# Stick-breaking attention inside a fused layer: value products issued two key blocks at a time, from two buffers of turned weights

## What is computed

```python
def stick_breaking_attention(q, k, v):          # 6 heads of 64, blocks of 128 queries
    for start in range(0, s_, Q_BLOCK):
        end = start + Q_BLOCK
        z = jnp.einsum('bqhd,bkhd->bhqk', q[:, start:end], k[:, :end]).astype(jnp.float32) * scale
        ...
        log_not = jnp.where(strict, jax.nn.log_sigmoid(-z), 0.0)
        tail = lax.cumsum(log_not, axis=3, reverse=True) - log_not
        weights = jnp.where(strict, jnp.exp(jax.nn.log_sigmoid(z) + tail), 0.0)
        outs.append(jnp.einsum('bhqk,bkhd->bqhd', weights.astype(v.dtype), v[:, :end]))

def ssd_chunked_scan(xs, dt, a, bm, cm):
    ...
    decay = jnp.where(causal, jnp.exp(jnp.where(causal, seg, 0.0)), 0.0)
```

## Time and profile before

| what | us |
|---|---|
| median of 3 runs | 1339.45 |
| lowest and highest of them | 1339.34, 1344.62 |
| the profiled execution, its own time | 1344.1 |
| its span in the trace | 1342.3 |
| the stretch of the attention's tasks | 71 to 354 |

### The profile page before, as it was taken

The page is one execution under the profiler, slowest core; times in us unless marked ns, Lnnn a source line. Parts: engine busy times, 40 slices in busy tenths (PEclk is TensorE's granted clock), DMA queues, the critical chain, the costliest instruction groups (busy, mean ns, idle before and its releaser), DMA issues.

```text
span 1342.3 us, 16727 instructions
## 1 busy us (share of the span) xinstructions
PE 1299.1 (97%) x6288; PEld 1027.5 (77%) x6288; DVE 841.8 (63%) x996; ACT 508.1 (38%) x778; POOL 227.7 (17%) x152
## 2 busy tenths in 40 slices
PE   6999999999989998999999999999999999999986
PEld 5776766777776887888888787878787787888886
DVE  4546645646388556423477777768676867677765
ACT  4435535547654225112333332424242333233421
POOL 0000000052310002500112111111112121211126
PEclk9999999999999998999999999999999999999998
DMA  5101000010003212111020111111120101011202
GB/s 232 47 32 32 32 32 32 32 48 16 1 16 111 79 49 95 60 32 47 16 79 32 63 40 55 47 47 63 47 77 33 63 31 63 31 63 47 94 32 95
DMA packets 22661, 71.97 MB, mean 54 GB/s; under 512 B 2512, under 2 KB 2768, under 8 KB 22608
## 3 DMA queue, kind: packets, MB, share of 16 engines
q1 hardware_dynamic: 22608, 71.22, 15.7%
HBM read 67.02 MB, written 4.19 MB: 53 GB/s over the span
## 4 chain that ended last, share of the span: by engine, by line
PE 72%; DVE 9%; ACT 3%; issue 2%; DMA 2%; DVEq 0%; SPq 0%; ACTq 0%
PE ps L696 13%; PE ps L698 13%; PE ps L697 13%; PE ps L1054 7%; PE ps L1055 7%; PE ps L1053 7%; PE ps L774 2%; PE ps L791 2%; DMA down_raw<-u_down 2%; DVE conv_ff L1864 1%; DVE w_lo L579 1%; PE ps L835 1%; PE ps L750 1%; ACT conv_ff L1454 1%; PE ps L1084 1%
## 5 line engine op out<-in xcount | busy, mean ns | idle before, releaser
L696 PE MATMUL ps<-x_hi,w_hi 128*128 128x512 f32 x336 | 140.1, 417 | 11.4 <-DVE x_lo L516 10.6
L698 PE MATMUL ps<-x_hi,w_lo 128*128 128x512 f32 x336 | 133.7, 398 | 0.0
L697 PE MATMUL ps<-x_lo,w_hi 128*128 128x512 f32 x336 | 133.5, 397 | 0.0
L1916 DVE TENSOR_TENSOR acc<-acc,ps 128x512 f32<-128x512 f32 x144 | 96.2, 685 | 53.0 <-PE ps L698 52.5
L1054 PE MATMUL ps<-mix_lo,w_hi 128*128 128x512 f32 x320 | 126.7, 396 | 0.0
L1053 PE MATMUL ps<-mix_hi,w_hi 128*128 128x512 f32 x320 | 126.7, 396 | 0.0
L1055 PE MATMUL ps<-mix_hi,w_lo 128*128 128x512 f32 x320 | 126.7, 396 | 0.0
L696 PE MATMUL ps<-h_hi,w_hi 128*128 128x512 f32 x288 | 114.8, 399 | 1.6 <-DVE acc L1916 1.6
L698 PE MATMUL ps<-h_hi,w_lo 128*128 128x512 f32 x288 | 114.1, 396 | 0.0
L697 PE MATMUL ps<-h_lo,w_hi 128*128 128x512 f32 x288 | 114.0, 396 | 0.0
L2191 POOL TENSOR_TENSOR weight_sums<-raw 128x512 f32<-128x512 f32 x20 | 29.1, 1456 | 494.2 <-DMA raw<-u_up 494.2
(11 more groups left out here) (263 smaller groups left out, 2841.5 us busy)
## 6 DMA issues: line engine op xcount, KB each, us to landing
raw<-u_up SPq DMA_DIRECT2D x44, 512.0 KB, 3.3
raw<-u_in SPq DMA_DIRECT2D x22, 512.0 KB, 3.3
down_raw<-u_down SPq DMA_DIRECT2D x40, 256.0 KB, 2.8
x_stage<-u_x SPq DMA_DIRECT2D x8, 512.0 KB, 7.8
raw<-u_out SPq DMA_DIRECT2D x8, 512.0 KB, 3.2
x_nat<-x_nat SPq DMA_DIRECT2D x8, 512.0 KB, 3.2
raw<-u_gate SPq DMA_DIRECT2D x8, 512.0 KB, 3.3
out<-o_norm SPq DMA_DIRECT2D x8, 512.0 KB, 2.6
```

Of the source, the lines that this page charges most:

```text
L696: mm(dst, w_hi, x_hi, start=first, stop=False)
L697: mm(dst, w_hi, x_lo, start=False, stop=False)
L698: return mm(dst, w_lo, x_hi, start=False, stop=last)
L1916: v.tensor_tensor(dst, dst, ps[:, DOWN_BANKS[k % 4], :], ALU.add).then_inc(dn_added, 1)
```

## The change

`values` of two key blocks are issued together. At a step behind a task with an odd kb nothing of `values` is issued; at the step behind the task with the even kb, the values of both follow each other. All blocks of 2k+2 tasks begin with an odd kb and end with kb = 0, so each is cut into pairs with nothing left over. The turned weights go to two buffers, chosen by kb modulo 2; the second lies where the mask lay, over `weight_sums`. The mask gets a place of its own with one 128x128 block, and the mask product reads it four times with a step of 0.

```diff
-    mask_r = put("mask", [P, 4, P], F32R, top[0] - 4 * HALF)
+    un_b = put("weights_t1", [P, HALF], F32, top[0] - 4 * HALF)
+    mask_r = put("mask", [P, P], F32R)
...
-    un = over("weights_t", [P, HALF], 19, F32, 21)
+    un = [over("weights_t0", [P, HALF], 19, F32, 21), un_b]
...
-                last = mm(ps[r, 7, q], vn[g % 2][:, kb, r], un[:, 2 * hd * P + q.start:2 * hd * P + q.stop],
+                last = mm(ps[r, 7, q], vn[g % 2][:, kb, r], un[kb % 2][:, 2 * hd * P + q.start:2 * hd * P + q.stop],
...
-            if t - 1 in TASK_AT:
+            if t - 1 in TASK_AT and BANK_TASKS[BANK_AT[t - 1]][4] % 2 == 0:
+                values(BANK_AT[t - 1] - 1)
                 values(BANK_AT[t - 1])
...
-                last = mm(dst[:, b * HALF:(b + 1) * HALF], ident_r[:, :], mask_r[:, :, :].rearrange("p k n -> p (k n)"),
-                          start=False, stop=True, skip_group_check=True)
+                last = mm(dst[:, b * HALF:(b + 1) * HALF].rearrange("p (k n) -> p k n", k=4), ident_r[:, :],
+                          mask_r[:, :].unsqueeze(1).broadcast_to([P, 4, P]), start=False, stop=True, skip_group_check=True)
...
-                act(pair(un[:, :]), pair(ps[:, 6, :]), ACT.Copy).then_inc(wt_out, 1)
+                act(pair(un[kb % 2][:, :]), pair(ps[:, 6, :]), ACT.Copy).then_inc(wt_out, 1)
...
-        v.tensor_scalar(mask_r[:, :, :], table("cap_le").unsqueeze(1).broadcast_to([P, 4, P]), 0.0, 32768.0, ALU.min,
-                        ALU.mult)
+        v.tensor_scalar(mask_r[:, :], table("cap_le"), 0.0, 32768.0, ALU.min, ALU.mult)
```

## The result

| | before | changed |
|---|---|---|
| median of 6 runs each | 1342.3 us | 1330.6 us |
| lowest and highest | 1339.34, 1344.62 | 1328.9, 1332.61 |
| ratio, 95% interval | | 0.9916 [0.9898, 0.9933] |
| span of the profiled execution | 1342.3 us | 1327.0 us |

The changed kernel is faster: by 11.7 us between the medians, and by 0.84% (11.3 us, interval 9.0 to 13.7 us) by the ratio of the runs, which is not formed from the two medians. The predicted time, 1330.7, is hit to 0.1 us, the predicted gain of 8.7 us is not: the three runs of the kernel before from which the prediction started had a low median. The profiled execution of the changed kernel is the fastest of its six.

A forecast was written before the change was run, and what follows sets the result against it. TensorE, busy for 97% of the span, was taken to bound the kernel. Savings of 3.7, 4.5 and 0.45 us, 8.7 in all, took the median from 1339.45 to 1330.7 us, chance 0.70, range 1327.5 to 1336.5.

The forecast's parts named there:

- What bounds the kernel: In the attention stage TensorE's slots set the end; a microsecond taken off there is worth one until another engine falls behind.
- The 0.30 us for a stay in the 128x64 shape: At visits with value products, changing into the 128x64 shape and out costs 0.30 us beyond turn and products.
- a turn alone at 0.44: Four transposes directly between projection matmuls cost only their columns, 0.44 us, at steps whose products are gone.
- Two sets in a row pay once: At visits with two sets of products, both pay for one shape change; the second adds only its columns.
- The row of SSD: SSD's half-width products L932 and L933, nearest evidence for two sets in a row: no gap between the groups.
- Step 20: Where scores stand ahead, the turn starts 0.58 us earlier; less 0.43 us, 0.15 us three times: 0.45 us gained.
- The sum: Gain over the attention stage's visits: 3.7 + 4.5 + 0.45 = 8.65, or 8.7 us.
- The mask and the buffers at zero: The mask's shorter build, its step-0 read in 12 mask products and the second buffer's place were each taken to change nothing.
- The rival with the slow read: Step of 0 makes the 12 mask products fetch columns one by one; at eight times the pitch 1350 us; chance 0.03.
- Waits and the other engine's chain: Stage waits cost and gain nothing; rival: ScalarE and VectorE chain bounds steps 17 to 28, half gain lost, 1335.1, chance 0.07.
- the step from the profile to the median: Profiled execution, 1344.1, lies 4.65 us over the median; the gain is taken from the median 1339.45.
- the term for all that lies behind the stage: Everything behind 354 us comes 8.7 us earlier with the same pauses; half clock may differ, 1.6 us either way each.

The follow-up runs named there:

- e2: Changed kernel with products at every step again, moved behind the step's first projection piece, away from the turn; ratio to the kernel before 1.0005.
- e4: Changed kernel with four key blocks' values together in the first pair of heads, two in the other pairs; median 1333.5 us, stage 298.57 us.
- e1: Changed kernel with the products issued at every step again, two buffers and one-block mask kept; ratio to the kernel before 0.9989.
- e8: Changed kernel with the last layer norm's two loads held back until the last down-projection weights have landed; median 1330.1 us.
- e9: Kernel before with the last layer norm's two loads held back until the last down-projection weights have landed; 1339.8 us, ratio 0.9971.
- the filled kernels: Changed kernel plus 19, 38 or 76 matmuls with unused result at the attention stage's end; medians 1339.7, 1342.55 and 1349.1 us.

## Why the prediction came out as it did

- **What bounds the kernel: right.** The visits fell by 8.51 us in all and the stage by 8.48, and TensorE's waits for VectorE stayed at 1.4 us in 3 places.
- **The 0.30 us for a stay in the 128x64 shape, and a turn alone at 0.44: right.** Measured 0.44 for the turn alone, and for a merged stay 1.39 and 1.60 us against 1.38 and 1.60. e2 shows that the price goes with the stay and not with the neighbour, e4 that a further stay saved is worth about as much (0.26 us). The Trainium skill, "TensorEngine Tiling (Array Packing)", Key Properties, says that a change of tiling mode drains TensorE and a change of tile alone does not. Both halves agree with the trace. The prediction took L698 and L761 as its case for the second half, but these stand in the same shape and the same tile; what bears it out is the two heads, which take turns in the two tiles of the 128x64 shape and cost 0.43 us for 256 columns each, their columns alone.
- **Two sets in a row pay once: right.** The row of SSD was the right one to take: 0.43 us more for 256 columns.
- **Step 20: right.** 0.58 us were taken off ahead of the turn: the visit went from 1.90 to 1.32 us.
- **The sum: 8.65 forecast, 8.48 measured** between the first scores and the barrier. 0.15 us of the difference is the one turn that cost 0.59 and not 0.44 us.
- **The mask and the buffers at zero: right,** shown by e1 and by the 0.60 us of the mask pair. The rival with the slow read falls.
- **Waits and the other engine's chain: right.** The rival falls by the 1.4 us that did not move; at most the 0.15 us of that one turn are a wait for another engine.
- **What failed: the step from the profile to the median, and the term for all that lies behind the stage.** I put the profiled execution 4.65 us over the median and took the median as given. It was that of three runs, two of which were low; in 63 runs the median is 1343.6, half a microsecond from the profiled execution's 1344.1. The second term I set at zero with 1.6 us either way for each half-clock stretch. The 1.6 us for a stretch was about right (1.64, 1.46 and 1.10 measured at the three places), the zero was not: the gain behind the stage is 11.7 - 8.5 = 3.2 us in the first comparison and about 4 over all runs, some 1 us of a shorter last pause and 2 to 3 us of half clock (0.0021 more mean clock at 1.1 us for each 0.001). The base was some 3 to 4 us too low and the gain 3 to 4 us too small, and these errors cancel: that the time was hit to 0.1 us is luck. The prediction says nothing of the last pause, since no edit touches it.
- **Still open:** why the clock is a little higher in the changed kernel beyond the tail. e8 and e9 still differ by 0.0008, which is within their errors; the filled kernels show no order. And the later landing named above.

## What to carry to other kernels

Where small matmuls in a narrower tile shape are scattered among full-width ones, count the stays in the other shape and not the matmuls: compare the start-to-start time of what stands between the full-width ones with its columns, and put work of one shape together if a spare buffer allows it. Full-shape transposes between full-shape matmuls cost only their columns. A gain taken from a stage should be checked at that stage's own landmarks, for the rest of the program moves by as much through its pauses and the clock; and a base of three runs is worth less than it looks.

## What the runs showed of the hardware

- Going from the 128x128 shape to 128x64 and back costs 0.30 us with a turn behind it and 0.35 us with projection behind it (e2: 0.78 us for 0.43 us of columns), at full clock; between float32r and float32 matmuls of one shape there is no such price (0.23 us from L699 to L775, and 1.61 us for 1.60 us of columns from L922 over the mask).
- A moving operand with a step of 0, four times 128 columns, streams at the rate of one with 512 columns of its own (0.60 us for two and the next start, either way).
- The same program after nearly the same pause was granted 2.4 GHz in one execution and 1.2 GHz in another. Over 63 runs of one kernel the mean clock varied from 0.989 to 0.995 and the span went with it, 1.1 us for 0.001, which makes most of the 9.6 us (1337.7 to 1347.3) that its runs differ by.
- Two 256 KB loads, issued up to 1.3 us ahead of two 512 KB loads that spread one row over all partitions, landed in 3.6 and 6.15 us; with the latter held back, in 3.0 and 3.7 (kernel before and e9).
